# Conditioning gate of the first MLP: products on VectorE over six blocks instead of matmuls over four

## The chip, the cores and the metric

One core of a Trainium2 chip (trn2) runs one program. The metric is the device time of that core in microseconds, the median of several executions, compared on the same chip. The engines are TensorE (PE), VectorE (DVE), ScalarE (ACT), GpSimd (POOL) and the sync engine (SP), whose queue issues most of the DMAs.

## The reference

Two layers of a sequence model on 256 tokens of width 2048, all in float32. The first layer is conditioned: six vectors of 2048 come from one row of conditioning `c`, and the last of them, `gt2`, weighs the output of the MLP:

```python
def adaln(cond, w, b):
    return jnp.split(jax.nn.silu(cond) @ w + b, 6, axis=-1)

def sq_relu_mlp(h, w1, w2):
    return jnp.square(jax.nn.relu(h @ w1)) @ w2

# in first_block
sh1, sc1, gt1, sh2, sc2, gt2 = adaln(c, w_mod[layer], b_mod[layer])
x_lat = x_lat + gt1[:, None] * rmsnorm(y_lat, norm_mix_post[layer])
h_lat = modulate(rmsnorm(x_lat, norm_mlp_pre[layer]), sh2[:, None], sc2[:, None])
x_lat = x_lat + gt2[:, None] * rmsnorm(sq_relu_mlp(h_lat, w_mlp_in[layer], w_mlp_out[layer]),
                                       norm_mlp_post[layer])
```

`w_mod` is 2048 x 12288; `gt2` needs its last 2048 columns (16 MB). The MLP is 2048 to 8192 to 2048. A second layer (convolution and spatial gating, then a Fourier mix, each with a SwiGLU) follows and isn't touched.

## The kernel before

**Units and blocks.** Every large product streams its weights as *units* of [128, 4, 512] float32, 1 MB, each one DMA into one of four slots of `raw`. Four units make a *block*: 2048 inputs times 512 outputs, for 256 tokens. `split` turns a unit into two parts: ACT writes the high part `w_hi` (L802), DVE the rest `w_lo` (L1069). PE multiplies a unit with 16 pairs of matmuls (L492 with `w_hi` on 512 columns, L493 with `w_lo` on 256), which accumulate in four of the eight PSUM banks, one half for even blocks and the other for odd ones. After a block DVE folds the banks into `tmp` (`fold`, L1075).

**What sets the order.** Each engine has its own hand-written order, tied by semaphores that count. SP loads unit u into its slot once `lo_ready` says that the slot's former unit has been split. ACT splits unit u when it has landed (`raw_ready`) and PE has used the slot's former `w_hi` (`pe_unit`). DVE follows ACT (`hi_ready`), PE follows DVE (`lo_ready`). PE starts block b when block b-2 has been folded. SP's and DVE's queues are in order: an instruction that waits holds all behind it.

**The stretch of the change.** The MLP has four parts (`MLP_PARTS`); in each, four blocks of the first product (`up`) are followed by four of the second (`down`). The first part, blocks c = 0 to 7 here, is written out. In loop step c, ACT and DVE split block c+1, then DVE folds block c (for c < 4 with the squared relu, ACT's copy into `hid` and DVE's low part L1094; for c >= 4 with an add to `y`, L1301). PE multiplies block c in step c.

**The conditioning units.** The gate's 16 MB are loaded in this stretch too, as 16 units (`late_gate`, L399): in each odd block c, once unit k of block c has been split, its slot takes unit k of gate part c // 2. Then SP waits until that has been used (`ada_unit`) before it loads the slot's unit of block c+1 (`late`, L385). PE uses them in the odd block itself (`late_rows`, L512): after its first unit, and once block c-1 has been folded, conditioning units 0 and 1; after its second, units 2 and 3. Four matmuls per unit multiply a column of `ada` (32 times the same) with 512 columns, into four groups of 32 partitions of bank 0. ACT copies the bank to `rs` (L815). After PE's third unit `late_columns` (L519) sums the four partitions `0, 32, 64, 96` with four matmuls of one column each, and ACT copies the result to `coef` (L818). PE waits for that copy (`ada_done`) before the next block.

The gate is used only after the last part of the MLP (L1415).

Of the kernel before, what the change touches and what calls it, by code (L numbers as in the profile page):

```python
# [10 lines left out]
ALU = mybir.AluOpType  # L11
# [76 lines left out]
def two_layer_kernel(nc, a, out):  # L88
    ctx = ExitStack()
    with ctx:  # L90
# [120 lines left out]
        coef_at = gm.at  # L211
        coef = gm("coef", [P, 3 * KT + 1])
        R_COL, X_COL, T_COL = 0, 2, 4
        x_mean = conv_tmp[:, 0, 0:2]
        eps_col = coef[:, 3 * KT:3 * KT + 1]
# [166 lines left out]
        def GEMM_SP(sp):  # L382
            def unit(u, slot, src, k, col, early=None, late=0):
                if late:
                    sp.wait_ge(ada_unit, ADA_UNITS + 4 * (late - 1) + slot + 1)  # L385
                if early is not None and early < SLOTS:
                    sp.wait_ge(ada_unit, ADA_UNITS - SLOTS + early + 1)
                else:
                    sp.wait_ge(lo_ready, u - (SLOTS - 1))
                sp.dma_start(raw[:, slot, :, :], src[:, ds(k * UK, UK), ds(col, UN)]).then_inc(raw_ready[slot], 16)  # L390

            def block_(u, src, col, k0=0, late=0):
                for k in range(4):
                    unit(u + k, k, src, k0 + k, col, late=late)

            def late_gate(i, u):
                for k in range(UK):
                    sp.wait_ge(lo_ready, u + k + 1)
                    sp.dma_start(raw[:, k, :, :], w_mod[:, k * UK:(k + 1) * UK, 2 * D + (KT - LATE + i) * UN:2 * D + (KT - LATE + i + 1) * UN]  # L399
                                 ).then_inc(raw_ready[k], 16)  # L400

# [8 lines left out]
            def glu(i):  # L410
                block_(8 * i, w_glu, i * UN)
                block_(8 * i + 4, w_glu, i * UN + D)
            with sp.Fori(1, 4) as i:
                glu(i)
            for c in range(2 * NCK):
                block_(MLP[0] + 4 * c, *((w_in, c * UN, 0) if c < NCK else (w_out, (c - NCK) * UN, 0)), late=c // 2)
                if c % 2:
                    late_gate(c // 2, MLP[0] + 4 * c)
            with sp.Fori(1, MLP_PARTS) as q:
                with sp.Fori(0, 4) as i:  # L420
                    block_(32 * q + (4 * i + MLP[0]), w_in, q * (4 * UN) + i * UN, late=LATE)
                with sp.Fori(0, 4) as i:
                    block_(32 * q + (4 * i + (MLP[0] + 16)), w_out, i * UN, q * 4)
# [45 lines left out]
        def GEMM_PE(pe):  # L469
            def block_(u, blk, half, operand, ready=None, units=4, slot0=0, between=None, after=1, order=None, narrow=False, piece=None, late=None):  # L470

# [4 lines left out]
                for k in range(units):  # L476
# [264 lines left out]
            for c in range(2 * NCK):  # L741
                if c and c % 2 == 0:
                    pe.wait_ge(ada_done, 1 + c // 2)
                block_(MLP[0] + 4 * c, MLP[1] + c, c % 2, *((xin, normed_from(0)) if c < NCK else (hid, hid_from(0))),
                       piece=first_from(0) if c == 0 else None, late=c // 2 if c % 2 else None)
            pe.wait_ge(ada_done, 1 + LATE)
# [49 lines left out]
        def GEMM_ACT(act):  # L796
# [8 lines left out]

            def split(grp, early=False, slots=range(SLOTS), late=LATE):

                for slot in slots:
                    split_unit(4 * grp + slot, slot, 16 * grp + 16 * (ADA_DMA + late + 1), early)

            def split_and_turn(grp, i):

                split(grp, slots=(0, 1), late=i + 1)
                act.wait_ge(ada_unit, ADA_UNITS + 4 * (i + 1))
                act.activation(rs[:, :, :].rearrange("p a t -> p (a t)"), ps[0], ACT.Copy).then_inc(ada_sb, 1)  # L815
                split(grp, slots=(2,), late=i + 1)
                act.wait_ge(ada_col, 5 + i + 1)
                act.activation(coef[:, 2 * KT + NT * i:2 * KT + NT * (i + 1)], ps[1][:, 0:NT], ACT.Copy).then_inc(ada_done, 1)  # L818
                split(grp, slots=(3,), late=i + 1)

# [16 lines left out]
            def seam(s, left=()):  # L837
                if s.post:
                    weigh(s.n, NCK - 1)
                    act.wait_ge(y_sum, s.n + 1)  # L840
                    mean_root(ps[0][:, 0:2], rs[:, 0, R_COL:R_COL + 2], y_root)
                    for grp in left:
                        split(grp, slots=(SLOTS - 1,), late=LATE * s.n)
# [85 lines left out]
            for i in range(4):  # L929
                for g in (2 * i + 1, 2 * i + 2):  # L930
                    split(g, slots=(0, 1) if g < 8 else (0,), late=0)
                    if g in (3, 4):
                        copy_x(g - 3)
                    if g == 5:
                        act.wait_ge(ms0_sum, 1)
                        act.activation(x_mean, ps[7][:, 0:2], ACT.Copy).then_inc(x_kept, 1)
                    if g == 7:
                        weigh(0, 0)
                        split(g, slots=(2,), late=0)
                        weigh(0, 1)  # L940
                        split(g, slots=(3,), late=0)
                        break
                    if g < 8:
                        split(g, slots=(2, 3), late=0)
# [4 lines left out]
            split(8, slots=(0, 1, 2), late=0)  # L949
            act.wait_ge(pe_unit, 32)  # L950
# [10 lines left out]
            for c in range(2 * NCK):  # L961
                if c % 2:
                    split_and_turn(G + 1 + c, c // 2)
                else:
                    split(G + 1 + c, late=c // 2)
                if c < NCK:
                    hidden(c, c, c % 2, hid)
# [94 lines left out]
        def GEMM_DVE(dve):  # L1062
# [342 lines left out]

            with dve.Fori(0, MLP_PARTS - 1) as q:
                up(q)
                dve.wait_ge(zeroed, 1)
# [1013 lines left out]
```

## Time and profile before

| | us |
|---|---|
| median of 3 runs | 3344.39 (3337.98 to 3345.87) |
| the profiled execution | 3345.34, its span 3343.4 |
| granted TensorE clock, mean | 0.969 |

| engine | busy us | share of the span |
|---|---|---|
| PE matmul | 3163.8 | 95% |
| PE weight load | 2763.9 | 83% |
| DVE | 2139.8 | 64% |
| ACT | 1434.8 | 43% |
| POOL | 325.9 | 10% |

The profile is one execution taken by the hardware profiler. Times are in us from the start of the span. A share of busy time is a mean over stages with different limits, so the stretch of the change, from about 640 to 850 us, is read by itself, in the timeline of each engine. "idle before" in a timeline row names the instruction whose end released the row. L12 is line 12 of the kernel. DMAs moved 643.63 MB, 193 GB/s in the mean.

### The profile page before, as it was taken

The page shows a single profiled execution, that of the slowest core. Times are in us where ns is not written, and L with a number is a line of the kernel's source. Part 1 is how long each engine was busy: PE and PEld are TensorE (multiplying, and loading weights), DVE is VectorE, ACT ScalarE, POOL GpSimd, SP SyncE. Part 2 cuts the span into 40 slices and gives each one's busy share as a digit, 9 for nine tenths or more (in the row PEclk, how much of TensorE's full clock was granted, in tenths as well). Part 3 has the DMA queues.
Part 4 walks back from the last instruction along what each step waited for, and adds up shares of the span by engine and source line. Part 5 has one row for each costly group of instructions (what it writes and reads, how often), then busy time and mean ns, then how long its engine had stood idle before and what let it go on. Part 6 is the DMA issues. An engine that isn't in the chain of part 4 may idle for free.

```text
span 3343.4 us, 54092 instructions
## 1 busy us (share of the span) xinstructions
PE 3163.8 (95%) x22493; PEld 2763.9 (83%) x22493; DVE 2139.8 (64%) x1892; ACT 1434.8 (43%) x1567; POOL 325.9 (10%) x227
## 2 busy tenths in 40 slices
PE   5878799899999999899899999999989999999998
PEld 3545578777888888899798888888989888888888
DVE  7878755855556656879666655656656666566565
ACT  4646543433333334476344434433334443443343
POOL 3989600000000000000000000000000000000000
PEclk7789999899999999999899999999999999999999
DMA  9698875376655565356155555555535555556552
GB/s 295 205 294 252 246 251 182 126 276 237 213 191 188 190 189 189 133 183 207 62 189 188 184 196 188 188 189 185 192 108 177 191 185 196 189 177 203 190 188 89
DMA packets 351056, 643.63 MB, mean 193 GB/s; under 512 B 21599, under 2 KB 50359, under 8 KB 350519
## 3 DMA queue, kind: packets, MB, share of 16 engines
q1 hardware_dynamic: 318400, 578.20, 52.7%
q10 hardware_dynamic: 32503, 63.21, 5.7%
q8 instruction: 118, 1.93, 0.2%
q14 instruction: 35, 0.29, 0.0%
HBM read 637.29 MB, written 4.06 MB: 192 GB/s over the span
## 4 chain that ended last, share of the span: by engine, by line
PE 85%; DVE 5%; DMA 4%; ACT 3%; issue 2%; SPq 1%; POOL 0%; ACTq 0%; DVEq 0%; POOLq 0%
PE acc L492 42%; PE acc L493 26%; PE acc L489 5%; PE acc L490 5%; PE acc L1662 2%; DMA raw<-in_w_mod_dram 1%; ACT u L1917 1%; DMA r_scratch<-rw 1%; DMA tw<-r_scratch 1%; PE acc L1754 1%; ACT w_hi L802 1%; DVE w_lo L1069 1%; PE acc L1737 1%; DVE tmp L1075 1%; DMA xs<-in_x_dram 1%
## 5 line engine op out<-in xcount | busy, mean ns | idle before, releaser
L1069 DVE TENSOR_TENSOR w_lo<-raw,w_hi 128x2048 fp32r<-128x2048 f32 x484 | 1104.9, 2291 | 931.7 <-ACT w_hi L802 929.8
L802 ACT ACTIVATE w_hi<-raw 128x2048 fp32r<-128x2048 f32 x484 | 923.3, 1914 | 1115.0 <-PE acc L493 1079.0
L492 PE MATMUL acc<-hid,w_hi 128*128 128x512 f32 x3776 | 1310.8, 392 | 0.0
L493 PE MATMUL acc<-xin,w_lo 128*128 128x256 f32 x3968 | 1113.3, 281 | 0.0
L493 PE MATMUL acc<-hid,w_lo 128*128 128x256 f32 x3840 | 1073.3, 280 | 0.0
L492 PE MATMUL acc<-xin,w_hi 128*128 128x512 f32 x2496 | 871.5, 393 | 5.6 <-DVE xin L1181 5.6
L492 PEld LDWEIGHTS acc<-hid,w_hi 128*128 128x128 f32 x3776 | 708.8, 188 | 159.7 <-issue 3.4
L493 PEld LDWEIGHTS acc<-xin,w_lo 128*128 128x128 f32 x3968 | 749.1, 189 | 0.0
L493 PEld LDWEIGHTS acc<-hid,w_lo 128*128 128x128 f32 x3840 | 720.8, 188 | 0.1
L492 PEld LDWEIGHTS acc<-xin,w_hi 128*128 128x128 f32 x2496 | 470.7, 189 | 114.0 <-issue 5.9
L489 PE MATMUL acc<-xin,w_hi 128*128 128x256 f32 x1472 | 414.9, 282 | 4.1 <-DVE xin L1183 2.2
L490 PE MATMUL acc<-xin,w_hi 128*128 128x256 f32 x1472 | 414.0, 281 | 0.0
L489 PEld LDWEIGHTS acc<-xin,w_hi 128*128 128x128 f32 x1472 | 278.7, 189 | 6.1 <-issue 3.2
L490 PEld LDWEIGHTS acc<-xin,w_hi 128*128 128x128 f32 x1472 | 278.6, 189 | 0.0
L1075 DVE TENSOR_REDUCE tmp<-acc 128x1024 f32<-128x2048 f32 x98 | 223.8, 2284 | 0.0
L1662 PE MATMUL acc<-raw,cond 128*32 128x512 f32 x640 | 96.7, 729 | 21.7 <-DMA raw<-in_w_mod_dram 21.7
L886 ACT ACTIVATE xin<-tmp 128x1024 f32 x22 | 23.3, 1061 | 158.0 <-DVE tmp L1321 158.0
L1662 PEld LDWEIGHTS acc<-raw,cond 128*32 128x32 f32 x640 | 19.1, 127 | 74.7 <-issue 41.3
L2320 POOL TENSOR_TENSOR cpow<-cpow,ptmp 128x1024 f32<-128x1024 f32 x32 | 75.3, 2354 | 1.3
L1536 POOL MEMSET conv_in<- 128x120 f32 x1 | 0.2, 204 | 750.5 <-DVE xr L1169 750.5
L1917 ACT ACTIVATE u<-acc,modt 128x32 f32<-128x32 f32 x256 | 70.8, 417 | 1.1 <-PE acc L1695 0.6
L900 ACT ACTIVATE tmp<-tmp 128x1024 f32<-128x1024 f32 x22 | 23.3, 1061 | 107.2 <-DVE tmp L1314 107.2
(314 smaller groups left out, 2242.8 us busy)
## 6 DMA issues: line engine op xcount, KB each, us to landing
raw<-in_ffn_w_gate_dram SPq DMA_DIRECT2D x88, 1024.0 KB, 5.2
raw<-in_ffn_w_up_dram SPq DMA_DIRECT2D x88, 1024.0 KB, 5.2
raw<-in_ffn_w_down_dram SPq DMA_DIRECT2D x88, 1024.0 KB, 5.2
raw<-in_w_mlp_in_dram SPq DMA_DIRECT2D x64, 1024.0 KB, 5.3
raw<-in_w_mlp_out_dram SPq DMA_DIRECT2D x64, 1024.0 KB, 5.2
raw<-in_w_mod_dram ACTq DMA_DIRECT2D x60, 1024.0 KB, 9.2
raw<-in_w_mod_dram SPq DMA_DIRECT2D x36, 1024.0 KB, 7.7
raw<-in_s_w_glu_dram SPq DMA_DIRECT2D x32, 1024.0 KB, 5.7
```

The source lines that it names most:

```text
L489: pe.matmul(bank[:, 0:TOK], w_hi[:, slot, w], operand[:, kt, 0:TOK], start=first, stop=False)
L490: pe.matmul(bank[:, 0:TOK], w_hi[:, slot, w], operand[:, kt, TOK:2 * TOK], start=False, stop=False)
L492: pe.matmul(bank, w_hi[:, slot, w], operand[:, kt, :], start=first, stop=False)
L493: ins = pe.matmul(bank[:, 0:TOK], w_lo[:, slot, w], operand[:, kt, 0:TOK], start=False, stop=last)
L802: act.activation(w_hi[:, slot, :], raw[:, slot, :, :].rearrange("p k n -> p (k n)"), ACT.Copy).then_inc(hi_ready, 1)
L1069: dve.tensor_tensor(w_lo[:, slot, :], raw[:, slot, :, :].rearrange("p k n -> p (k n)"), w_hi[:, slot, :].bitcast(F32), SUB).then_inc(lo_re ...
L1075: dve.tensor_reduce(dst, acc[:, 4 * half:4 * half + 4, :].rearrange("p a (t b) -> p a b t", t=2), AX.X, ADD).then_inc(folded, 1)
L1662: ins = pe.matmul(ps[0][32 * q:32 * q + 32, :], cond[:, kk * UK + q, window:window + 32], raw[:, kk, q, :], start=(m + kk == 0), stop=(kk ...
L1737: ins = pe.matmul(ps[1 + ri][s * NST:(s + 1) * NST, cb * 64:(cb + 1) * 64], ew[:, ri, cb, s * NST:(s + 1) * NST], uv[:, :, ::-1] if d else ...
L1754: ins = pe.matmul(o, st[s * NST:(s + 1) * NST, ri, 4 * d + kp, :], cpow[cp][s * NST:(s + 1) * NST, ri, 4 * d + kp, :], start=False, stop=( ...
L1917: ins = act.activation(u[b][:, g, q * NCH:(q + 1) * NCH], ps[6][:, g * 64 + q * NCH:g * 64 + (q + 1) * NCH], ACT.Identity, bias=modt[:, 16 ...
L2320: return pool.tensor_tensor(o, x, y, op)
```

## The change

The conditioning units are multiplied by DVE. For each unit, `late_products` runs four instructions on [128, 512]: row q of the unit times a column of `ada` (one scalar per partition), added to a running sum in `gate_sum` (the buffers `rs` and `conv_tmp` in turn). Each waits for the one before (`x_step.settle`). The sum then has all 128 partitions, and `late_columns` sums them on PE, with the same four matmuls against a column of ones.

The 16 units are spread over six blocks instead of four (`LATE_AT`): part 0 in blocks 1 (units 0, 1) and 2 (units 2, 3), part 1 in blocks 3 and 4, part 2 in block 5, part 3 in block 6. In DVE's step c the products of a block's first two units stand ahead of the split of slot 0, the others ahead of the split of the next slots. The column matmuls stand after PE's second unit of blocks 3, 5, 6 and 7 (`LATE_TURN`), in the bank of the half that the block doesn't use, so they wait for the fold of the block before. ACT copies their result after its second split of the step, and PE waits for it before the next block.

DVE's loop over the first three parts becomes this written-out first part and a loop over two. `x_mean` moves from `conv_tmp` to `coef`.

```diff
+        LATE_AT = {1: (0, (0, 1)), 2: (0, (2, 3)), 3: (1, (0, 1)), 4: (1, (2, 3)), 5: (2, (0, 1, 2, 3)), 6: (3, (0, 1, 2, 3))}
+        LATE_TURN = {3: 0, 5: 1, 6: 2, 7: 3}
...
         def GEMM_SP(sp):
             def unit(u, slot, src, k, col, early=None, late=0):
                 if late:
-                    sp.wait_ge(ada_unit, ADA_UNITS + 4 * (late - 1) + slot + 1)
+                    sp.wait_ge(ada_unit, ADA_UNITS + late)
...
+            def late_gate(c):
+                i, units = LATE_AT[c]
+                for k in units:
+                    sp.wait_ge(lo_ready, MLP[0] + 4 * c + k + 1)
+                    sp.dma_start(raw[:, k, :, :], w_mod[:, k * UK:(k + 1) * UK, 2 * D + (KT - LATE + i) * UN:2 * D + (KT - LATE + i + 1) * UN]
+                                 ).then_inc(raw_ready[k], 16)
+
             for c in range(2 * NCK):
-                block_(MLP[0] + 4 * c, *((w_in, c * UN, 0) if c < NCK else (w_out, (c - NCK) * UN, 0)), late=c // 2)
-                if c % 2:
-                    late_gate(c // 2, MLP[0] + 4 * c)
+                for k in range(4):
+                    i, units = LATE_AT.get(c - 1, (0, ()))
+                    unit(MLP[0] + 4 * c + k, k, w_in if c < NCK else w_out, k, c % NCK * UN, late=4 * i + k + 1 if k in units else 0)
+                if c in LATE_AT:
+                    late_gate(c)
...
         def GEMM_PE(pe):
-                    if late is not None and k < 2:
-                        if k == 0:
-                            pe.wait_ge(folded, blk)
-                        late_rows(late, blk - MLP[1], (2 * k, 2 * k + 1))
-                    if late is not None and k == 2:
-                        late_columns(late)
...
-            def late_columns(i):
-                pe.wait_ge(ada_sb, 5 + i + 1)
+            def late_columns(c):
+                i, bank = LATE_TURN[c], ps[4 * (1 - c % 2)]
+                pe.wait_ge(folded, MLP[1] + c)
+                pe.wait_ge(ada_unit, ADA_UNITS + 4 * (i + 1))
                 for r in range(NT):
-                    ins = pe.matmul(ps[1][:, r:r + 1], rs[:, r // 2, r % 2 * P:(r % 2 + 1) * P], one_of_32, start=True, stop=True)
+                    ins = pe.matmul(bank[:, r:r + 1], gate_sum[i % 2][:, r * P:(r + 1) * P], ones[:, 0:1], start=True, stop=True)
                 ins.then_inc(ada_col, 1)
...
         def GEMM_DVE(dve):
+            def late_products(c, k):
+                i, to = LATE_AT[c][0], gate_sum[LATE_AT[c][0] % 2]
+                if k == 0 and i > 1:
+                    dve.wait_ge(ada_col, 5 + i - 1)
+                dve.wait_ge(raw_ready[k], 16 * (ADA_UNITS // SLOTS + MLP[0] // SLOTS + c + 1 + late_loads(k, c) + 1))
+                for q in range(UK):
+                    row, weight = raw[:, k, q, :], ada[:, 3 * KT + k * UK + q:3 * KT + k * UK + q + 1]
+                    if q:
+                        x_step.settle()
+                    elif k:
+                        dve.wait_ge(ada_unit, ADA_UNITS + 4 * i + k)
+                    if k + q:
+                        ins = dve.scalar_tensor_tensor(to, row, weight, to, MUL, ADD)
+                    else:
+                        ins = dve.tensor_scalar(to, row, weight, None, MUL)
+                    if q < UK - 1:
+                        x_step(ins)
+                ins.then_inc(ada_unit, 1)
+
+            for c in range(2 * NCK):
+                left = list(LATE_AT.get(c, (0, ()))[1])
+                for k in range(SLOTS):
+                    for _ in range(2 if left and left[0] == 0 else 1):
+                        if left:
+                            late_products(c, left.pop(0))
+                    split(G + 1 + c, (k,))
+                if c < NCK:
...
+                    fold(MLP[0] + 4 * c + 4, c % 2, tmp[:, c % 2])
...
+                    hidden(c, c, c % 2, hid)
+                else:
...
+                    add_block(y, MLP[0] + 4 * c + 4, MLP[1] + c, c % 2, c - NCK, Y_MLP + c - NCK, NCK + 1)
```

## Rows read from the trace of the kernel before

**Rows 1.** The page, busy us, share of the span and instructions

```profile
PE 3163.8 (95%) x22493; PEld 2763.9 (83%) x22493; DVE 2139.8 (64%) x1892; ACT 1434.8 (43%) x1567; POOL 325.9 (10%) x227
```

**Rows 2.** Windows: us, busy per engine, PE clock, DMA share, GB/s

```profile
700.00:800.00 100.00, 97.91 (x589) 80.70 (x588) 53.11 (x27) 34.88 (x24) 0.00 (x0) 1.00 0.72 250
800.00:900.00 100.00, 98.96 (x584) 84.35 (x583) 54.67 (x29) 34.86 (x21) 0.00 (x0) 1.00 0.67 220
```

**Rows 3.** Timeline of DVE: start, duration, line, op [idle before, releaser]

```profile
674.05 1.23 DVE L1094 TENSOR_TENSOR hid<-tmp,hid 128x1024 f32 x1 [1.36 <-ACT hid L886]
...
719.64 2.28 DVE L1075 TENSOR_REDUCE tmp<-acc 128x1024 f32<-128x2048 f32 x1
...
747.95 2.29 DVE L1075 TENSOR_REDUCE tmp<-acc 128x1024 f32<-128x2048 f32 x1
...
770.13 2.28 DVE L1075 TENSOR_REDUCE tmp<-acc 128x1024 f32<-128x2048 f32 x1
772.59 1.23 DVE L1301 TENSOR_TENSOR y<-y,tmp 128x1024 f32 x1 [0.17 <-DVE tmp L1075]
```

**Rows 4.** Timeline of PE in block 3, around its conditioning matmuls

```profile
720.65 0.28 PE L493 MATMUL acc<-xin,w_lo 128*128 128x256 f32 x1
721.98 1.92 PE L512 MATMUL acc<-raw,ada 128*32 128x512 f32 x16 [1.04 <-DVE tmp L1075]
723.83 0.50 PE L492 MATMUL acc<-xin,w_hi 128*128 128x512 f32 x1
...
737.09 0.95 PE L519 MATMUL acc<-consts,rs 128*128 128x1 f32 x8
```

**Rows 5.** Groups of DVE by form: busy us, mean ns of one

```profile
L1446 DVE SCALAR_TENSOR_TENSOR z<-conv_in,par,z 128x256 f32<-128x256 f32 x120 | 48.2, 479 | 0.0
...
L2016 DVE TENSOR_TENSOR bpow<-bpow,acc 128x512 f32<-128x512 f32 x64 | 43.5, 680 | 0.6
...
L1398 DVE SCALAR_TENSOR_TENSOR tmp<-tmp 128x1024 f32<-128x1024 f32 x16 | 19.6, 1226 | 0.6
```

**Rows 6.** Timeline of DVE in the first layer's mixer, one settled step after another

```profile
309.36 0.67 DVE L2016 TENSOR_TENSOR bpow<-bpow,acc 128x512 f32<-128x512 f32 x1
310.07 0.70 DVE L2016 TENSOR_TENSOR acc<-acc,bb 128x512 f32<-128x512 f32 x1
310.68 0.68 DVE L2016 TENSOR_TENSOR bpow<-acc,bb 128x512 f32<-128x512 f32 x1
```

**Rows 7.** Loads of weights (L390), then conditioning (L399): issue to landing

```profile
DMA to landing us min/median/max: 5.1/7.0/9.8
...
DMA to landing us min/median/max: 4.8/5.3/7.4
```

**Rows 8.** Timeline of SP's queue: the load that follows conditioning unit 0

```profile
723.10 0.37 SPq L390 DMA_DIRECT2D raw<-in_w_mlp_out_dram  x1
```

**Rows 9.** Timeline of ACT: splits that wait for loads, and one for block 7

```profile
728.32 1.92 ACT L802 ACTIVATE w_hi<-raw 128x2048 fp32r<-128x2048 f32 x1 [4.04 <-DMA raw<-in_w_mlp_out_dram]
730.98 1.92 ACT L802 ACTIVATE w_hi<-raw 128x2048 fp32r<-128x2048 f32 x1 [0.74 <-DMA raw<-in_w_mlp_out_dram]
...
844.78 1.92 ACT L802 ACTIVATE w_hi<-raw 128x2048 fp32r<-128x2048 f32 x1 [4.47 <-PE acc L493]
```

**Rows 10.** Windows around PE waits and in busy DMA stretches, columns as rows 2

```profile
624.00:641.00 17.00, 10.49 (x36) 9.08 (x37) 15.81 (x35) 7.15 (x11) 0.00 (x0) 0.50 0.30 100
1587.00:1596.80 9.80, 3.14 (x7) 2.52 (x8) 9.38 (x20) 3.19 (x2) 0.00 (x0) 0.50 0.01 5
...
666.00:671.00 5.00, 4.44 (x26) 3.66 (x24) 4.06 (x2) 0.91 (x1) 0.00 (x0) 1.00 1.01 340
...
736.00:741.00 5.00, 5.00 (x34) 4.50 (x33) 1.71 (x1) 1.97 (x2) 0.00 (x0) 1.00 1.05 389
```

**Rows 11.** Timeline of PE: the two waits of the half clock

```profile
626.05 1.01 PE L544 MATMUL acc<-consts,q_h 128*128 128x1 f32 x4 [4.59 <-DVE q_h L1131]
...
1593.66 3.35 PE L582 MATMUL acc<-tmp,consts 128*128 128x256 f32 x7 [10.52 <-ACT tmp L1019]
```

More of the change, by code:

```diff
@@ L211, in two_layer_kernel @@
         coef_at = gm.at
-        coef = gm("coef", [P, 3 * KT + 1])
+        coef = gm("coef", [P, 3 * KT + 3])
         R_COL, X_COL, T_COL = 0, 2, 4
-        x_mean = conv_tmp[:, 0, 0:2]
+        x_mean = coef[:, 3 * KT + 1:3 * KT + 3]
+        gate_sum = [v[:, :, :].rearrange("p a t -> p (a t)") for v in (rs, conv_tmp)]
         eps_col = coef[:, 3 * KT:3 * KT + 1]
@@ L313, in two_layer_kernel, with late_loads @@
         ADA_UNITS, LATE = 32 + 3 * KT, KT // 4
+        LATE_AT = {1: (0, (0, 1)), 2: (0, (2, 3)), 3: (1, (0, 1)), 4: (1, (2, 3)), 5: (2, (0, 1, 2, 3)), 6: (3, (0, 1, 2, 3))}
+        LATE_TURN = {3: 0, 5: 1, 6: 2, 7: 3}
+        def late_loads(slot, block):
+            return sum(slot in units for c, (_, units) in LATE_AT.items() if c < block)
         FF = a["ffn_w_gate_2"].shape[2]
@@ L390, in unit, with block_ @@
                 sp.dma_start(raw[:, slot, :, :], src[:, ds(k * UK, UK), ds(col, UN)]).then_inc(raw_ready[slot], 16)
-            def block_(u, src, col, k0=0, late=0):
+            def block_(u, src, col, k0=0):
                 for k in range(4):
[L394 to L400, printed above, removed]
+                    unit(u + k, k, src, k0 + k, col)
             for k in range(4):
@@ L414, in GEMM_SP @@
                 glu(i)
-            for c in range(2 * NCK):
-                block_(MLP[0] + 4 * c, *((w_in, c * UN, 0) if c < NCK else (w_out, (c - NCK) * UN, 0)), late=c // 2)
-                if c % 2:
-                    late_gate(c // 2, MLP[0] + 4 * c)
+            def late_gate(c):
[4 more added lines that the diff above has]
+                                 ).then_inc(raw_ready[k], 16)
+            for c in range(2 * NCK):
+                for k in range(4):
[3 more added lines that the diff above has]
+                    late_gate(c)
             with sp.Fori(1, MLP_PARTS) as q:
                 with sp.Fori(0, 4) as i:
-                    block_(32 * q + (4 * i + MLP[0]), w_in, q * (4 * UN) + i * UN, late=LATE)
+                    block_(32 * q + (4 * i + MLP[0]), w_in, q * (4 * UN) + i * UN)
                 with sp.Fori(0, 4) as i:
@@ L469, in GEMM_PE, with block_ @@
         def GEMM_PE(pe):
-            def block_(u, blk, half, operand, ready=None, units=4, slot0=0, between=None, after=1, order=None, narrow=False, piece=None, late=None):
+            def block_(u, blk, half, operand, ready=None, units=4, slot0=0, between=None, after=1, order=None, narrow=False, piece=None):
                 if not isinstance(blk, int):
@@ L741, in GEMM_PE @@
             for c in range(2 * NCK):
-                if c and c % 2 == 0:
-                    pe.wait_ge(ada_done, 1 + c // 2)
+                if c - 1 in LATE_TURN:
+                    pe.wait_ge(ada_done, 2 + LATE_TURN[c - 1])
                 block_(MLP[0] + 4 * c, MLP[1] + c, c % 2, *((xin, normed_from(0)) if c < NCK else (hid, hid_from(0))),
-                       piece=first_from(0) if c == 0 else None, late=c // 2 if c % 2 else None)
+                       piece=first_from(0) if c == 0 else None, between=(lambda c=c: late_columns(c)) if c in LATE_TURN else None)
             pe.wait_ge(ada_done, 1 + LATE)
@@ L804, in GEMM_ACT, with split @@
             ADA_DMA = ADA_UNITS // SLOTS
-            def split(grp, early=False, slots=range(SLOTS), late=LATE):
+            def split(grp, early=False, slots=range(SLOTS), block=2 * NCK):
                 for slot in slots:
[L809 to L819, printed above, removed]
+                    split_unit(4 * grp + slot, slot, 16 * grp + 16 * (ADA_DMA + late_loads(slot, block) + 1), early)
             def weigh(n, c):
@@ L842, in seam @@
                     for grp in left:
-                        split(grp, slots=(SLOTS - 1,), late=LATE * s.n)
+                        split(grp, slots=(SLOTS - 1,), block=2 * NCK * s.n)
                     act.wait_ge(x_ms, s.n + 1)
@@ L930, in GEMM_ACT @@
                 for g in (2 * i + 1, 2 * i + 2):
-                    split(g, slots=(0, 1) if g < 8 else (0,), late=0)
+                    split(g, slots=(0, 1) if g < 8 else (0,), block=0)
                     if g in (3, 4):
@@ L938, in GEMM_ACT @@
                         weigh(0, 0)
-                        split(g, slots=(2,), late=0)
+                        split(g, slots=(2,), block=0)
                         weigh(0, 1)
-                        split(g, slots=(3,), late=0)
+                        split(g, slots=(3,), block=0)
                         break
                     if g < 8:
-                        split(g, slots=(2, 3), late=0)
+                        split(g, slots=(2, 3), block=0)
                 if i < 3:
@@ L948, in GEMM_ACT @@
             weigh(0, NCK - 2)
-            split(8, slots=(0, 1, 2), late=0)
+            split(8, slots=(0, 1, 2), block=0)
             act.wait_ge(pe_unit, 32)
@@ L961, in GEMM_ACT @@
             for c in range(2 * NCK):
-                if c % 2:
-                    split_and_turn(G + 1 + c, c // 2)
+                if c in LATE_TURN:
+                    i = LATE_TURN[c]
+                    split(G + 1 + c, slots=(0, 1), block=c + 1)
+                    act.wait_ge(ada_col, 5 + i + 1)
+                    act.activation(coef[:, 2 * KT + NT * i:2 * KT + NT * (i + 1)], ps[4 * (1 - c % 2)][:, 0:NT], ACT.Copy).then_inc(ada_done, 1)
+                    split(G + 1 + c, slots=(2, 3), block=c + 1)
                 else:
-                    split(G + 1 + c, late=c // 2)
+                    split(G + 1 + c, block=c + 1)
                 if c < NCK:
@@ L1404, in down @@
                           4 * q + (2 * i + (Y_MLP + j)), 4 * q + 5)
-            with dve.Fori(0, MLP_PARTS - 1) as q:
+            def late_products(c, k):
[24 more added lines that the diff above has]
+                if c < NCK:
+                    dve.wait_ge(y_added, Y_MLP)
+                    dve.wait_ge(hid_ready, c + 1)
+                    fold(MLP[0] + 4 * c + 4, c % 2, tmp[:, c % 2])
+                    dve.wait_ge(folded, MLP[1] + c + 1)
+                    dve.scalar_tensor_tensor(tmp[:, c % 2], tmp[:, c % 2], 0.0, tmp[:, c % 2], ALU.max, MUL).then_inc(h_ready, 1)
+                    hidden(c, c, c % 2, hid)
+                else:
+                    if c == NCK:
+                        dve.wait_ge(zeroed, 1)
+                    add_block(y, MLP[0] + 4 * c + 4, MLP[1] + c, c % 2, c - NCK, Y_MLP + c - NCK, NCK + 1)
+            with dve.Fori(1, MLP_PARTS - 1) as q:
                 up(q)
-                dve.wait_ge(zeroed, 1)
                 with dve.Fori(0, 2) as i:
```

10 lines of the change are left out of this document (removed).

## Prediction

> **What bounds the kernel now.** I read the page's busy times first, then the windows, then the timelines of one engine at a time. The page has PE busy 95% of the span and DVE 64% [rows 1]. The change touches only eight blocks of weights (four of the first MLP product, four of the second) that run from about 643 to 845 us. The windows there have PE at 98 to 99%, DVE at 53 to 55%, the DMA share at 0.72 and 0.67 and the clock at 1.00 [rows 2]. So TensorE bounds this stretch. Its pace is read at DVE's fold, which follows each block [rows 3]: 719.64 to 747.95 is 28.3 us, 747.95 to 770.13 is 22.2 us; the pattern repeats four times. Every odd block is 6.1 us longer than a plain one, and a plain one is 4 units of 5.55 us.
>
> The PE timeline shows the 6.1 us [rows 4]. After the first unit of an odd block PE waits 1.04 us for a fold and runs 16 conditioning matmuls in 1.92 us: the last w_lo matmul starts at 720.65, the next of the stream would at 720.77 and does at 723.83, and its own pair is 0.1 longer, 3.2 us in all. The column matmuls after the third unit take 0.95 us, some 0.9 more than none. The rest of the 6.1, 2.0 us, is the second batch of 16, after the second unit, without a wait. Four times 6.1 is 24.5 us of 3345.34.
>
> **The change, part by part.**
> *Removed from PE:* the 128 row matmuls with their wait, (3.2 + 2.0) x 4 = 21 us. The column matmuls stay, same shape, same 0.9 us each in blocks 3, 5, 6 and 7. If nothing else were late PE would gain 21 us. *Removed from ACT:* a 0.57 us copy per gate, in idle time: nothing.
>
> *Added to DVE:* 16 units of products, each 4 instructions on 128x512, each waiting for the one before. No such row exists. DVE takes 479 ns for scalar_tensor_tensor 128x256 with a column as scalar, 680 ns for 128x512 and 1226 ns for 128x1024 without one [rows 5]; 512 more elements cost 0.546 us, so 256 more cost 0.27 and the new one takes 0.75 us. Bounds of the start to start: between settled instructions the gap was 0.03 us (309.36 + 0.67 to 310.07), between unsettled ones they overlap by 0.09 (310.07 + 0.70 to 310.68) [rows 6], and after a fold the add starts 0.17 late (770.13 + 2.28 to 772.59) [rows 3]. That is 0.67 to 0.92; I take 0.78, by the settled pair. A unit is then 3.1 us, all of them 50 us. DVE idles 92 us of the 200 from 700 to 900 [rows 2], so the sum would fit. The order is what matters.
>
> *Moved:* a conditioning unit lies in a raw slot. SP loads the slot's next weight unit only when the product is done, and SP's queue is in order, so every later load is behind that wait. DVE's queue is in order too: in a block it does product 0, product 1, split of unit 0, and in the two four-unit blocks also product 2, split 1, product 3, splits 2 and 3, and the fold last. Split 0 waits for ACT, which waits for the load, which waits for product 0. One round trip is: DMA to landing 5.1 us at least, 7.0 in the median (most of those with others in flight) [rows 7]; ACT started at 728.32, 5.2 us after SP's issue at 723.10, and the next load was there 2.66 us later, at 730.98 [rows 8, 9]; then ACT 1.92 us and DVE's split 2.2 us. Before, this chain starts once per odd block, after 1.9 us of PE work, and has a whole 28 us block to catch up.
>
> I carry DVE's queue forward from its last instruction of block 0, which ends at 675.28 [rows 3], with those durations: product 3.1 (a unit that starts with a plain multiply 3.0), load 5.3, ACT 2.0, split 2.2, loads behind each other 2.7 apart, tail of a first-product block (fold 2.3, square 1.3, ACT 1.1, low part 1.4) 6.1, of a second-product block (fold, add) 3.6.
> - Block 1 (units 0, 1): product 0 ends at 3.0, the loads land at 8.3, 11.4, 14.1, 16.8, the last split ends at 21.1, tail: 27.2 us. Block 3 the same.
> - Block 2 (units 2, 3): product 2 at 3.1; split 0 ends at 6.3, since its load left only behind two conditioning loads; product 3 at 9.4, its slot's load at 14.6, last split 19.0, tail: 25.1. Block 4 has the short tail: 22.7.
> - Blocks 5 and 6 (four units): product 0 at 3.0, its slot filled at 8.3, split 0 ends at 12.5; product 2 at 15.7, split 1 at 17.9, product 3 at 21.0, its slot filled at 26.3, split 3 ends at 30.5, tail: 34.2 each. Two round trips one after the other, on a queue that must turn within 22.2.
>
> Sum 170.6: DVE is through block 6 at 845.9, its fold at 844.6. PE's column matmuls in block 7 stand after its second unit and wait for that fold (their bank is block 6's); behind them in PE's queue are half a block, so PE ends block 7 at 844.6 + 0.9 + 11.1 = 856.6. Before, ACT's split that waits for that same end starts at 844.78 [rows 9], so 844.7. The loss is **+12 us**. The 21 us that PE gives back are all spent in waits. After block 7 both kernels run PE at 22.2 us a block, with nothing that could take the loss back.
>
> *The fold wait:* before, it came after one unit and cost 1.04 us; now after two, but DVE folds last, so in blocks 5, 6 and 7 it is what ends PE's idle time, some 8 us in each of the last two. *The clock:* in the kernel before, the PE waits of 4.6 and 10.5 us each have a stretch at half clock with them (624 to 641 and 1587 to 1596.8, granted clock 0.50, which is 1.2 GHz), and the second goes on for 3.1 us after PE has resumed at 1593.66 [rows 10, 11]. After the 1.04 us waits it stays at 1.00, 2.4 GHz [rows 2]. A wait of 8 us before block 7's second half should leave some 5.4 us of half clock on the path, of which half is lost: +2.7, bounds 0 and 8.5 (the 17 us stretch). Earlier stretches fall where PE waits for DVE anyway. *Other edits* (x_mean moved into coef, the constant dropped, DVE's first pass unrolled) add no instruction to a path: nothing; what hides a stall of code fetching is DVE's own wait for a load, 4 us before each split 0 above, and without that cover it would add itself.
>
> **What the skill says of one term.** The round trip rests on the load's 5.2 us, a row. The Trainium skill, "DMA: Bandwidth & Descriptors", section "Anatomy of one DMA — SWDGE (gpsimd) path", fits a DMA at about 2.0 us plus bytes over 436 GB/s, an estimate of 4.4 us for 1 MB. By it the eight trips on the path would be 0.8 us shorter each and the loss some 6 us smaller; no load here is that quick, the shortest took 4.8 us [rows 7].
>
> **Sum.** 3345.34 (the profiled execution; span 3343.4) + 12 + 2.7 = 3360.0. The profiled execution is 0.95 above the median 3344.39, so the median forecast is 3359.1 us. Bounds: 48 of the 64 product instructions are on DVE's path, at 0.67 or 0.92 instead of 0.78 that is -5 or +7; loads 3.1 instead of 2.7 apart (340 GB/s in the window at 666, against 389 at 736 [rows 10]) +6; trips -1 to +3; clock -2.7 to +6.
>
> **Rivals.**
> - *The cover holds:* products fall into DVE's idle time, loads stay ahead, PE gains its 21 us: 3344.39 - 21 = 3323. For it: DVE's 92 us idle against 50 added [rows 2]. It decides where SP stands: if the loads behind a product left early enough that DVE's turn stayed under 22.2 us in blocks 5 and 6. The break-even is a total of 158 us for the six blocks instead of 170.6. Against it: 34.2 is made of durations each of which has a row. Chance 0.13.
> - *Short links:* the same chain with products at 0.67 to 0.72, no clock loss: +3 to +9, about 3350. Chance 0.22.
> - *Forecast:* +10 to +21, 3359. Chance 0.52.
> - *Long links:* loads 3.1 apart, the half clock lasting as at 624: +22 to +30, about 3370. Chance 0.13.
> That the change doesn't take the work off PE is no case: the row matmuls are gone from its program.
>
> **How the numbers follow.** A measurement of this kernel can tell about 0.3%, 10 us. Slower by more: 0.52 and 0.13, less a little at the forecast's lower edge, 0.63. Within: 0.22 and the edges, 0.24. Faster: 0.13. The range leaves out the fast rival and the last of the long one: 3346 to 3374.
>
> **What would show it.** In the profile after: no 128*32 matmuls with ada; scalar_tensor_tensor 128x512 x60 of about 0.75 us; the folds of blocks 5 and 6 about 34 us apart, those of blocks 1 to 4 22 to 28; PE idle some 8 us twice before column matmuls, with DVE's fold as releaser; ACT waiting 7 us or more for raw; half clock near 840; from block 8 on 22.2 us per block. Wrong if folds 5 and 6 are under 26 us apart (then the first rival), if the new instruction is outside 0.67 to 0.92, or if the loss arises outside these eight blocks.

## The result, and the profile after

| | before | after |
|---|---|---|
| median of 6 runs each, us | 3343.41 (3337.98 to 3345.87) | 3355.12 (3351.87 to 3356.34) |
| ratio | | 1.0036 [1.0023, 1.0049] |
| profiled execution, us | 3345.34, span 3343.4 | 3351.87, span 3350.1 |

The change costs 11.7 us, 0.36%. The forecast was +14.7.

The page of the kernel after: busy us, share of the span, instructions. PE is busy 11.7 us less than in [rows 1], DVE 44 us more, and the kernel is longer.

```profile
PE 3152.1 (94%) x22365; PEld 2767.7 (83%) x22365; DVE 2183.8 (65%) x1956; ACT 1432.8 (43%) x1563; POOL 325.9 (10%) x227
```

The new instruction, from the answer for its line (count: shortest/median/longest in ns, first and last start in us):

```profile
L1406 DVE SCALAR_TENSOR_TENSOR rs<-raw,ada,rs x30: 745/752/753, 670.7 to 791.8; 128x512 f32<-128x512 f32 x30
L1406 DVE SCALAR_TENSOR_TENSOR conv_tmp<-raw,ada,conv_tmp x30: 744/752/754, 723.5 to 825.3; 128x512 f32<-128x512 f32 x30
```

Four of them take 3.11 us (the rows with "x4" below), 0.78 each. DVE's timeline of the kernel after, block 5 (L1408 and L1406 are the products, L1057 is the split, L1063 the fold, L1289 the add to `y`; in brackets the idle time ahead and what ended it). Block 5 is an odd block, of 28.3 us before (as 719.64 to 747.95 in [rows 3]); block 6 is a plain one, of 22.2:

```profile
772.05 0.48 DVE L1408 TENSOR_SCALAR rs<-raw,ada 128x512 f32<-128x512 f32 x1
772.57 5.54 DVE L1406 SCALAR_TENSOR_TENSOR rs<-raw,ada,rs 128x512 f32<-128x512 f32 x7
782.05 2.29 DVE L1057 TENSOR_TENSOR w_lo<-raw,w_hi 128x2048 fp32r<-128x2048 f32 x1 [3.94 <-ACT w_hi L796]
784.25 3.11 DVE L1406 SCALAR_TENSOR_TENSOR rs<-raw,ada,rs 128x512 f32<-128x512 f32 x4
787.28 2.28 DVE L1057 TENSOR_TENSOR w_lo<-raw,w_hi 128x2048 fp32r<-128x2048 f32 x1
789.49 3.11 DVE L1406 SCALAR_TENSOR_TENSOR rs<-raw,ada,rs 128x512 f32<-128x512 f32 x4
794.62 2.29 DVE L1057 TENSOR_TENSOR w_lo<-raw,w_hi 128x2048 fp32r<-128x2048 f32 x1 [2.03 <-ACT w_hi L796]
799.81 2.29 DVE L1057 TENSOR_TENSOR w_lo<-raw,w_hi 128x2048 fp32r<-128x2048 f32 x1 [2.89 <-ACT w_hi L796]
802.02 2.28 DVE L1063 TENSOR_REDUCE tmp<-acc 128x1024 f32<-128x2048 f32 x1
...
805.48 0.48 DVE L1408 TENSOR_SCALAR conv_tmp<-raw,ada 128x512 f32<-128x512 f32 x1
...
835.40 2.28 DVE L1063 TENSOR_REDUCE tmp<-acc 128x1024 f32<-128x2048 f32 x1
...
857.43 2.28 DVE L1063 TENSOR_REDUCE tmp<-acc 128x1024 f32<-128x2048 f32 x1
...
879.61 2.29 DVE L1063 TENSOR_REDUCE tmp<-acc 128x1024 f32<-128x2048 f32 x1
```

From the first product of block 5 to that of block 6 are 33.4 us, and the folds of blocks 5 and 6 (802.02, 835.40) are as far apart. DVE idles 8.9 of them, in three waits for ACT. What ACT waited for stands in its own timeline, its splits of the same block's units:

```profile
780.10 1.92 ACT L796 ACTIVATE w_hi<-raw 128x2048 fp32r<-128x2048 f32 x1 [13.74 <-DMA raw<-in_w_mlp_out_dram]
783.31 1.92 ACT L796 ACTIVATE w_hi<-raw 128x2048 fp32r<-128x2048 f32 x1 [1.30 <-DMA raw<-in_w_mlp_out_dram]
...
792.67 1.92 ACT L796 ACTIVATE w_hi<-raw 128x2048 fp32r<-128x2048 f32 x1 [7.39 <-DMA raw<-in_w_mlp_out_dram]
797.87 1.91 ACT L796 ACTIVATE w_hi<-raw 128x2048 fp32r<-128x2048 f32 x1 [3.27 <-DMA raw<-in_w_mlp_out_dram]
```

and SP's queue shows why the loads are late: four loads of one block take 18 us to issue, since the later two wait for products that DVE does only after splits 0 and 1.

```profile
774.92 18.07 SPq L394 DMA_DIRECT2D raw<-in_w_mlp_out_dram  x4
```

The price is paid on PE. Its timeline of the kernel after, all six waits of over 0.5 us in the stretch; [rows 4] has the same kinds of row of before:

```profile
719.55 1.87 PE L513 MATMUL acc<-consts,rs 128*128 128x1 f32 x8 [3.37 <-DVE tmp L1063]
...
736.36 0.50 PE L499 MATMUL acc<-hid,w_hi 128*128 128x512 f32 x1 [1.96 <-ACT coef L950]
...
770.93 1.05 PE L513 MATMUL acc<-consts,conv_tmp 128*128 128x1 f32 x8 [1.02 <-DVE tmp L1063]
...
785.34 0.50 PE L499 MATMUL acc<-hid,w_hi 128*128 128x512 f32 x1 [0.58 <-ACT coef L950]
...
804.36 1.87 PE L513 MATMUL acc<-consts,rs 128*128 128x1 f32 x8 [7.65 <-DVE tmp L1063]
...
837.74 1.87 PE L513 MATMUL acc<-consts,conv_tmp 128*128 128x1 f32 x8 [7.20 <-DVE tmp L1063]
```

Windows of the kernel after (us, then busy us and instructions of PE, PEld, DVE, ACT, POOL, then granted TensorE clock, DMA share, GB/s): the four stretches at half clock, the whole stretch from DVE's first product to PE's end of block 7. The last row is the same stretch of the kernel before.

```profile
718.30:725.10 6.80, 5.55 (x20) 4.97 (x21) 5.55 (x6) 1.06 (x1) 0.00 (x0) 0.50 0.01 3
772.90:776.30 3.40, 3.40 (x13) 2.92 (x12) 3.19 (x5) 0.00 (x0) 0.00 (x0) 0.51 0.58 182
800.30:810.50 10.20, 6.14 (x22) 5.48 (x23) 9.88 (x10) 0.00 (x0) 0.00 (x0) 0.50 0.85 300
834.40:844.60 10.20, 6.86 (x24) 6.09 (x25) 8.91 (x5) 3.86 (x3) 0.00 (x0) 0.50 0.92 316
670.17:853.20 183.03, 160.89 (x871) 140.19 (x871) 131.48 (x107) 55.31 (x34) 0.00 (x0) 0.92 0.73 253
...
675.28:844.70 169.42, 166.29 (x1000) 136.86 (x999) 86.05 (x42) 56.86 (x38) 0.00 (x0) 1.00 0.75 260
```

These rows balance the account. The kernel before went through the same stretch (DVE's end of block 0 at 675.28, PE's end of block 7 at 844.7) in 169.4 us; its window 675.28 to 844.70 has PE busy 166.3, all at full clock, and idle 3.1. After, it is 183.0: PE is busy 160.9 and idle 22.1. Of the 160.9, 21.95 us ran at half clock, so 11.0 were lost and the work itself is worth 149.9. Work -16.4, idle time +19.0, half clock +11.0: **+13.6 us**. The work did go, as the change says, and more than its worth came back as waiting and as lower clock. (Of the 11.0 only the last 3.4 lengthen the kernel, worked out below. Each of the three earlier ones is followed by another wait of PE, of 1.96, 0.58 and 7.20 us, which would otherwise have been longer.)

### The profile page after: what moved, and what is told of

The parts are those of the page before. It is cut to its first block, busy times and chain, and to the rows that moved or that the text cites. A ratio compares the mean times of both kernels' runs of the same rounds, so it can differ in the third digit from the quotient of the medians.

```text
span 3350.1 us, 53806 instructions
## 1 busy us (share of the span) xinstructions
PE 3152.1 (94%) x22365; PEld 2767.7 (83%) x22365; DVE 2183.8 (65%) x1956; ACT 1432.8 (43%) x1563; POOL 325.9 (10%) x227
## 4 chain that ended last, share of the span: by engine, by line
PE 80%; DVE 7%; DMA 5%; ACT 4%; issue 2%; POOL 1%; SPq 1%; ACTq 0%; DVEq 0%; POOLq 0%
PE acc L499 40%; PE acc L500 25%; PE acc L496 5%; PE acc L497 5%; PE acc L1686 1%; DMA raw<-in_w_mlp_out_dram 1%; DMA raw<-in_w_mod_dram 1%; ACT w_hi L796 1%; ACT u L1941 1%; PE acc L1778 1%; DMA r_scratch<-rw 1%; DVE w_lo L1057 1%; DMA raw<-in_w_mlp_in_dram 1%; DMA tw<-r_scratch 1%; DVE tmp L1063 1%
## 5 line engine op out<-in xcount | busy, mean ns | idle before, releaser
L1057 DVE TENSOR_TENSOR w_lo<-raw,w_hi 128x2048 fp32r<-128x2048 f32 x484 | 1104.8, 2292 | 897.8 <-ACT w_hi L796 895.9
L1063 DVE TENSOR_REDUCE tmp<-acc 128x1024 f32<-128x2048 f32 x98 | 223.8, 2284 | 0.0
```

Of the source, the lines that this page charges most:

```text
L1057: dve.tensor_tensor(w_lo[:, slot, :], raw[:, slot, :, :].rearrange("p k n -> p (k n)"), w_hi[:, slot, :].bitcast(F32), SUB).then_inc(lo_re ...
L1063: dve.tensor_reduce(dst, acc[:, 4 * half:4 * half + 4, :].rearrange("p a (t b) -> p a b t", t=2), AX.X, ADD).then_inc(folded, 1)
```

## The experiments

The theory on trial: what costs the time is the *order*. A product stands on DVE's queue ahead of the split that DVE owes PE, and the load for that split can't leave before the product is done. The rivals are DVE's added work itself (50 us), the traffic of the 16 MB in their new places, and PE's new wait for the fold. Experiment 1 changes the order alone, 2 takes the work away, 3 moves the wait, and 4 and 5 keep work and traffic and change only which slots the units lie in. Ratios are against the kernel before, on the same chip.

**1. All products of a block ahead of its first split.** Same work, same loads, another order on DVE in blocks 2, 4, 5 and 6.

```diff
-                    for _ in range(2 if left and left[0] == 0 else 1):
+                    for _ in range(len(left)):
```

> The changed kernel with one edit: in DVE's queue all products of a block stand ahead of the first split, also those of units 2 and 3, which stood behind splits 0 and 1 (blocks 2, 4, 5, 6). Same instructions, same loads, same 50 us of DVE work. Theory (one round trip of load, ACT, split behind the last product instead of two in a row): DVE's turn in blocks 5 and 6 is products 12.2, load 5.3, ACT 2.0, split 2.2, tail 3.6 = 25.3 us instead of 33.4 measured after the change; blocks 2 and 4 lose 3 us each. Time about 12 us below the kernel before, 23 below the changed one: 3332. Rival A (DVE has too much work): the same work, so no change from the changed kernel, 3355. Rival B (DMA traffic of six blocks slows the loads): the same traffic, 3355.

Measured: 3331.28 us (before 3341.86), ratio 0.9972 [0.9962, 0.9983]; -10.6 us. It goes from slower than before to faster by one line of DVE's order. DVE's timeline of this kernel, block 5:

```profile
765.75 0.48 DVE L1408 TENSOR_SCALAR rs<-raw,ada 128x512 f32<-128x512 f32 x1
766.27 11.99 DVE L1406 SCALAR_TENSOR_TENSOR rs<-raw,ada,rs 128x512 f32<-128x512 f32 x15
778.18 6.69 DVE L1057 TENSOR_TENSOR w_lo<-raw,w_hi 128x2048 fp32r<-128x2048 f32 x3
785.68 2.29 DVE L1057 TENSOR_TENSOR w_lo<-raw,w_hi 128x2048 fp32r<-128x2048 f32 x1 [0.82 <-ACT w_hi L796]
...
791.35 0.48 DVE L1408 TENSOR_SCALAR conv_tmp<-raw,ada 128x512 f32<-128x512 f32 x1
```

The turn is 25.6 us instead of 33.4, and of the 8.9 us of idle time 0.8 are left: while DVE does products 1, 2 and 3, the loads behind product 0 arrive. SP issues the four loads in 10.0 us instead of 18.1. Blocks 1 and 3, whose order this edit leaves as it was, still take 27.3 and 26.6.

**2. Hardly any product work.** The order of the kernel after, but each product is one instruction on 16 columns (the plain multiply that opens a gate part stays on 512). This leaves out nearly all of the gate's sum, so `coef` is not the reference's.

```diff
-                for q in range(UK):
+                for q in range(1):
...
-                        ins = dve.scalar_tensor_tensor(to, row, weight, to, MUL, ADD)
+                        ins = dve.scalar_tensor_tensor(to[:, 0:16], row[:, 0:16], weight, to[:, 0:16], MUL, ADD)
...
-                    if q < UK - 1:
-                        x_step(ins)
```

> The changed kernel with each unit's product cut to one instruction, on 16 of 512 columns (for unit 0 the one plain multiply on 512): the gate's sum is left out but for a scrap, its loads and waits stay. DVE loses about 47 of the 50 us. Theory: the products on the path go, but in blocks 5 and 6 product 2 still stands behind split 0 and its load behind it, two trips in a row: DVE's turn there is still 25 to 26 us, and the time about 18 us below the kernel before, 3325. Rival A (work): all of PE's gain, 21 below, 3322. Rival B (traffic): loads stay slow, 3345 to 3355.

Measured: 3333.08 us (before 3341.86), ratio 0.9969 [0.9958, 0.998]. The gain is 8.8 us by the medians, half of what I expected, and no more than experiment 1 has with all 50 us of product work in it. A part of what is missing is in the timelines of this kernel, block 5, of DVE, then of SP's queue and ACT:

```profile
761.47 0.23 DVE L1406 SCALAR_TENSOR_TENSOR rs<-raw,ada,rs 128x16 f32<-128x16 f32 x1
770.08 2.29 DVE L1057 TENSOR_TENSOR w_lo<-raw,w_hi 128x2048 fp32r<-128x2048 f32 x1 [8.38 <-ACT w_hi L796]
...
779.90 2.29 DVE L1057 TENSOR_TENSOR w_lo<-raw,w_hi 128x2048 fp32r<-128x2048 f32 x1 [4.80 <-ACT w_hi L796]
783.15 2.29 DVE L1057 TENSOR_TENSOR w_lo<-raw,w_hi 128x2048 fp32r<-128x2048 f32 x1 [0.96 <-ACT w_hi L796]
...
761.39 14.10 SPq L394 DMA_DIRECT2D raw<-in_w_mlp_out_dram  x4
...
768.13 1.92 ACT L796 ACTIVATE w_hi<-raw 128x2048 fp32r<-128x2048 f32 x1 [12.95 <-DMA raw<-in_w_mlp_out_dram]
```

DVE sits idle 14 us of a 27.9 us turn. Both round trips are still there; that they are short of work makes them no shorter. Nor was the first one 5.3 us from issue to ACT: SP issued at 761.39 and ACT started at 768.13, 6.7 us. The four conditioning loads had been issued from 748.40 to 757.91, and part of them was still in flight: from 757.9 to 761.4 the DMA share is 1.04, with 387 GB/s. So PE still waits 2.97 and 2.75 us for the folds. The work does count in this order, since it stands in series with the trips: its removal is worth 20.5 us, from +11.7 to -8.8. But as much comes back in experiment 1 with the work left in, and experiment 6 below, again with all of it, is 12.8 us better than this kernel. DVE's work as such is not the cost. My forecast of the size was wrong in part because it took the load's time from a quieter moment: the turns of blocks 5 and 6 are 27.9 and 27.7 us instead of 25 to 26, which is 4 to 5 of the 9 us that are missing; and behind each of PE's two waits there are some 3.4 us at half clock (granted clock 0.52 from 789 to 792.4 and from 816 to 819.5). What the rest is stays open.

**3. Column matmuls one unit later.** The wait for the fold then has one unit less behind it; ACT's copy to `coef` stays behind its second split.

```diff
-                       piece=first_from(0) if c == 0 else None, between=(lambda c=c: late_columns(c)) if c in LATE_TURN else None)
+                       piece=first_from(0) if c == 0 else None, between=(lambda c=c: late_columns(c)) if c in LATE_TURN else None, after=2)
```

> The changed kernel with PE's column matmuls, and the wait for the fold in front of them, moved from behind the second unit of the block to behind the third. Theory (DVE's queue is the bound, the fold wait only where PE's lateness shows): one unit more is done before the wait, but ACT's copy of the result comes later, so what is won in block 7 is lost at the starts of blocks 4 and 7: within 5 us of the changed kernel, 3350 to 3360. Rival C (the wait for the fold, with the half clock behind it, is the cost): 8 us of idle time before blocks 6's and 7's columns shrink to 2.5 and the half clock goes: 3340 to 3345.

Measured: 3347.84 us (before 3341.86), ratio 1.002 [1.0011, 1.0029]: +6 us, between the two expectations. DVE's turns of blocks 5 and 6 are 33.4 us each, as in the kernel after. From DVE's first product to its fold of block 8 are 201.5 us (674.52 to 876.06) instead of 209.4 in the kernel after and 195.8 before. My expectation had ACT's copy behind its third split, too; as it stands, the copy blocks ACT's later splits, and PE's waits move from the fold to `coef`. In PE's timeline of this kernel, before the first matmuls of blocks 4 and 7:

```profile
740.65 0.79 PE L499 MATMUL acc<-hid,w_hi 128*128 128x512 f32 x1 [8.07 <-ACT coef L950]
...
823.85 0.79 PE L499 MATMUL acc<-hid,w_hi 128*128 128x512 f32 x1 [6.02 <-ACT coef L950]
```

The waits for the folds of blocks 5 and 6 shrink to 1.58 and 0.42 us, but the waits for `coef` take their place, so this experiment by itself doesn't settle that rival. Experiment 1 does: its column matmuls stand where those of the kernel after stand, and PE has no wait of over 0.3 us for a fold in these blocks.

What follows here is only this: where on PE the wait stands is worth some 6 us, about one unit (5.5 us), and moving it in this way makes the loss smaller but doesn't turn it.

**4 and 5. Which slots hold the products.** Both have experiment 1's order in all blocks. In blocks 1 to 4 the two conditioning units lie either in slots 2 and 3, whose splits come last, or in slots 0 and 1, whose splits come first. Work, traffic and PE's program are the same in both.

The table now gives (unit, slot); SP's waits and the counts follow from it. First experiment 4, then 5 (their other edits only read the new table, and are the same in both):

```diff
-        LATE_AT = {1: (0, (0, 1)), 2: (0, (2, 3)), 3: (1, (0, 1)), 4: (1, (2, 3)), 5: (2, (0, 1, 2, 3)), 6: (3, (0, 1, 2, 3))}
+        LATE_AT = {1: ((0, 2), (1, 3)), 2: ((2, 2), (3, 3)), 3: ((4, 2), (5, 3)), 4: ((6, 2), (7, 3)), 5: ((8, 0), (9, 1), (10, 2), (11, 3)), 6: ((12, 0), (13, 1), (14, 2), (15, 3))}
...
```

```diff
+        LATE_AT = {1: ((0, 0), (1, 1)), 2: ((2, 0), (3, 1)), 3: ((4, 0), (5, 1)), 4: ((6, 0), (7, 1)), 5: ((8, 0), (9, 1), (10, 2), (11, 3)), 6: ((12, 0), (13, 1), (14, 2), (15, 3))}
...
```

> As e1 (all products of a block ahead of its first split), and in blocks 1 and 3 the two conditioning units are put into slots 2 and 3 instead of 0 and 1, as they are in blocks 2 and 4. Same products, loads and matmuls; only the slots differ. Theory (what costs is a product in front of the load that DVE's next split needs): slots 0 and 1 of the next block are loaded before the products end, DVE's turns in blocks 1 and 3 fall from 26.5 to about 22, only blocks 5 and 6 stay at 25: 16 to 20 us below the kernel before, 6 to 9 below e1: 3323 to 3326. Rival A (DVE's work) and rival B (DMA traffic): as e1, 3331.

> As e4 with the opposite choice: in blocks 1 to 4 the two units lie in slots 0 and 1. Same products, loads and matmuls. Theory: DVE's turns in blocks 1 to 4 are all 24 to 27 us, none has a margin: 2 us below to 4 above the kernel before, 3340 to 3346, some 20 us above e4. Rivals A and B: as e1, 3331.

Measured: slots 2 and 3 3322.95 us, ratio 0.9948 [0.9934, 0.9962], -19.7; slots 0 and 1 3342.02 us, ratio 1.0003 [0.9993, 1.0014], -0.7 (before 3342.68). Nineteen microseconds lie between two programs that differ in slot numbers only. DVE's timelines of block 1, first with slots 2 and 3, then with 0 and 1:

```profile
672.95 0.48 DVE L1411 TENSOR_SCALAR rs<-raw,ada 128x512 f32<-128x512 f32 x1
673.47 5.54 DVE L1409 SCALAR_TENSOR_TENSOR rs<-raw,ada,rs 128x512 f32<-128x512 f32 x7
678.93 6.92 DVE L1059 TENSOR_TENSOR w_lo<-raw,w_hi 128x2048 fp32r<-128x2048 f32 x3
```

```profile
674.17 0.48 DVE L1411 TENSOR_SCALAR rs<-raw,ada 128x512 f32<-128x512 f32 x1
674.69 5.54 DVE L1409 SCALAR_TENSOR_TENSOR rs<-raw,ada,rs 128x512 f32<-128x512 f32 x7
684.17 2.29 DVE L1059 TENSOR_TENSOR w_lo<-raw,w_hi 128x2048 fp32r<-128x2048 f32 x1 [3.94 <-ACT w_hi L799]
```

With slots 2 and 3, DVE goes from its products straight into three splits; the loads behind the products have 6.9 us of splits to hide under. With slots 0 and 1 DVE waits 3.94 us, and then 2.6 more in three rests. The turns of blocks 1 to 4 are 22.2, 22.2, 23.1, 19.8 against 27.4, 27.6, 27.1, 24.7. The traffic is the same in both, in the same blocks, so it is not the cause either.

**6. Seven blocks.** As experiment 4, with never more than three units in a block: blocks 5 and 6 take three each (slots 1 to 3), block 7 two. `LATE_TURN` names, for a block, the unit of PE's behind which the columns of a gate part stand.

```diff
+        LATE_AT = {1: ((0, 2), (1, 3)), 2: ((2, 2), (3, 3)), 3: ((4, 2), (5, 3)), 4: ((6, 2), (7, 3)), 5: ((8, 1), (9, 2), (10, 3)), 6: ((11, 1), (12, 2), (13, 3)), 7: ((14, 2), (15, 3))}
+        LATE_TURN = {3: {1: 0}, 5: {1: 1}, 6: {2: 2}, 7: {2: 3}}
...
```

> As e4, with the units over seven blocks: two each in slots 2 and 3 of blocks 1 to 4 and 7, three each in slots 1 to 3 of blocks 5 and 6; column matmuls in block 3 and 5 after the second unit, in 6 and 7 after the third. Theory: no turn of DVE is over 23 us, so PE keeps all its gain but the four column sums: 20 us below the kernel before, 3321 to 3323. Rival A (50 us of DVE work must cost): about e1, 3331. Rival D (the loads can't go faster than PE takes them in this stretch, whatever the order): not under 3327.

Measured: 3321.09 us (before 3342.68), ratio 0.9946 [0.9932, 0.996], -21.6 us: faster than both kernels, and the 21 us that PE was to give back, with every product done. Its windows:

```profile
660.00:720.00 60.00, 60.00 (x351) 52.94 (x350) 51.92 (x43) 22.38 (x13) 0.00 (x0) 1.00 0.84 286
720.00:760.00 40.00, 40.00 (x232) 35.20 (x231) 34.85 (x26) 14.55 (x9) 0.00 (x0) 1.00 0.85 297
760.00:800.00 40.00, 40.00 (x239) 35.44 (x238) 35.95 (x31) 15.47 (x10) 0.00 (x0) 1.00 0.85 290
800.00:850.00 50.00, 50.00 (x292) 43.98 (x292) 34.73 (x23) 16.09 (x10) 0.00 (x0) 1.00 0.82 278
```

PE is busy in all of it, at full clock, with DVE busy 87 to 90% of the first three windows and the DMA share at 0.82 to 0.85, where the kernel after had 0.73 over its stretch. The column matmuls stand in PE's stream without a wait:

```profile
789.22 0.28 PE L500 MATMUL acc<-hid,w_lo 128*128 128x256 f32 x1
789.33 0.95 PE L516 MATMUL acc<-consts,rs 128*128 128x1 f32 x8
790.15 0.48 PE L499 MATMUL acc<-hid,w_hi 128*128 128x512 f32 x1
```

## Why the prediction was right, point by point

- *PE's freed work.* Forecast 24.5 us less 3.6 for the columns, 4.2 of it waits, so 16.7 of work. Measured 16.4. Experiment 6 gets the whole of it: 21.6.
- *A product.* Forecast 0.78 us start to start, from the settled pair of [rows 6]; measured 0.78. The estimate by size from [rows 5], 0.75, is the duration (752 ns).
- *DVE's turns.* Forecast and measured, from the first product or split of one block to the next:

| block | 1 | 2 | 3 | 4 | 5 | 6 | sum |
|---|---|---|---|---|---|---|---|
| forecast | 27.2 | 25.1 | 27.2 | 22.7 | 34.2 | 34.2 | 170.6 |
| measured | 27.4 | 25.5 | 26.7 | 22.4 | 33.4 | 33.4 | 168.7 |

Within block 5, counted from its start: product 0 done, forecast 3.0, measured 2.9 (SP's issue); its slot's load split by ACT from 8.3, measured 8.1; split 1 done at 17.9, measured 17.5; product 3's slot with ACT at 26.3, measured 25.8. The two round trips are there. The 0.8 us by which the turn is shorter come in steps of 0.1 to 0.4 at each link, and none stands out. (The forecast's own links of these blocks, 30.5 and 3.6, add up to 34.1; its 34.2 is a rounding.)
- *The load's time.* Issue to ACT was 5.2 us at 774.92 to 780.10 and 5.2 to 5.3 at the next trips, as [rows 8, 9] had it. The Trainium skill, "DMA: Bandwidth & Descriptors", section "Anatomy of one DMA — SWDGE (gpsimd) path", gives an estimate of 4.4 for 1 MB, by which the loss would have been some 6 us smaller. That fit is for DMAs that GpSimd issues and these are issued by SP; the traces have no load of 4.4 us here, and with others in flight the load was slower still (6.7 us in experiment 2).
- *PE's end.* From the fold's end in block 6 to PE's end of block 7: forecast 0.9 + 11.1 + 2.7 = 14.7 us, measured 837.7 to 853.2, 15.5. The clock's share was 3.4, not 2.7: half clock lasts 6.9 us behind the wait instead of 5.4, a figure that no row gave and that I had put between the rows' bounds. The column matmuls run in it as well, 1.87 instead of 0.95 us.
- *The waits.* Forecast "some 8 us in each of the last two": 7.65 and 7.20, both ended by the fold. PE's smaller waits for `coef` (1.96, 0.58) I had not named; they fell in blocks where DVE was the later one.
- *The sum.* In the stretch the forecast was +14.7 and the trace has +13.6; the 1.9 us of shorter turns and the 0.8 of longer clock make up the difference. The medians differ by 11.7. The last 1.9 us are outside these blocks or chance. The two profiled executions themselves differ by 6.7 us in span: the one after reaches the stretch 5.1 us earlier (DVE's first product at 670.17, against 675.28) and takes 1.8 us less behind it. That start lies at 669.3 to 674.5 in the experiments, which do the same up to there. From it to DVE's fold of block 8 the experiments take, in their order, 184.8, 186.3, 201.5, 177.2, 196.7 and 175.4 us, against 195.8 before: -11.0, -9.5, +5.7, -18.7, +0.9 and -20.4, where the medians have -10.6, -8.8, +6.0, -19.7, -0.7 and -21.6. So the time is won and lost in this stretch, to within 2 us, and the moved `x_mean` and the written-out pass, which all of them have, cost nothing that shows outside it.
- *The chances.* The first rival (cover holds, 3323, 0.13) did not happen, but its mechanism is what experiments 4 and 6 have, at 3323 and 3321: "if the loads behind a product left early enough". The break-even of 158 us for six turns holds: 145.5 us in experiment 1, 10.6 us faster than before, and 157.4 in experiment 5, whose time is that of the kernel before to 0.7 us.
- *The margin.* The mechanism and its size were right, but the sign's margin is thin: the measured 0.36% lies just beyond the 0.3% that the prediction says a measurement can tell, and 2 us less would have lain within it.

## What to carry to other kernels

Before moving work onto an engine with idle time, write down what its in-order queue does in one turn and where each load that it waits for is released. If the moved work frees the buffer of the load that the *next* step needs, each such step pays a whole round trip (here load 5.2, ACT 1.9 and DVE 2.2 us), however little work it is. Put the moved work ahead of steps whose data are already there, and let it free the buffers that are needed last: the same 50 us of products then cost nothing.

## What I had not expected of the hardware

- **There was more half clock than I reckoned.** Four stretches in these blocks of the kernel after, 30.6 us, 21.95 of them with PE at work: PE's waits of 7.65 and 7.20 us each have a stretch of 10.2 us at a granted clock of 0.50 (1.2 GHz), the wait of 3.37 us one of 6.8, and one of 3.4 us (772.9) follows a wait of 1.02 us at 770.93, though [rows 2] have none after waits of 1.04 us. In experiment 6, where PE has no wait of over 0.3 us from 660 us on, the clock stays at 1.00 from 660 to 850 us. The length of the wait alone doesn't decide: waits of 2.00 and 2.21 us in experiment 5 have a stretch of 3.4 us each, waits of 2.26 us in experiment 1 and 2.04 in experiment 3 have none. What does decide was not tried.
- **A load's time depends on what is still in flight.** It took 5.2 us from issue to ACT in the kernel after, where the last conditioning load was issued 6 us earlier (by 769.07, the weight load at 774.92), and 6.7 us in experiment 2, where it was issued 3.5 us earlier (by 757.91, the weight load at 761.39) and the DMA share was 1.04 in between.
- **An engine at 90% can still be off the path.** In experiment 6 DVE is busy 35.95 us of the 40 from 760 to 800, and PE waits in none of them.
